# Input norm by token tiles with early first weights, and time steps from 16 stationary columns

## What is computed

```python
h = jnp.concatenate([meta, x], axis=1)            # 16 + 512 tokens
u = rmsnorm(h, norm_mix_w[l])                     # y = x * rsqrt(mean(x*x) + 1e-5) * w
proj = u @ w_in[l]                                # 1024 -> 5136 columns
z, xbc, dt_raw, conf_in = jnp.split(proj, [1024, 3072, 3088], axis=-1)
dt = jax.nn.softplus(dt_raw + dt_bias)            # 16 "time steps" per token, one per head
```

## Time and profile before

| | |
|---|---|
| Median of 3 runs | 3473.9 us (3464.41 to 3475.84) |
| The profiled execution, its own time | 3469.46 us |
| Its span, first to last instruction | 3467.0 us |
| Mean granted TensorE clock | 0.953 |
| Busy: PE, DVE, ACT, POOL | 92%, 77%, 52%, 21% of the span |
| Norm stage ends, projection stage starts | 31.71 us, 32.47 us |
| First matmul of the projection | 44.89 us |

### The profile page before, as it was taken

The page is one execution under the profiler, slowest core; times in us unless marked ns, Lnnn a source line. Parts: engine busy times, 40 slices in busy tenths (PEclk is TensorE's granted clock), DMA queues, the critical chain, the costliest instruction groups (busy, mean ns, idle before and its releaser), DMA issues. The chain is left out here.

```text
span 3467.0 us, 48111 instructions
## 1 busy us (share of the span) xinstructions
PE 3181.1 (92%) x16551; PEld 2746.6 (79%) x16551; DVE 2685.4 (77%) x3820; ACT 1815.5 (52%) x2180; POOL 738.5 (21%) x460
## 2 busy tenths in 40 slices
PE   5999778999897999999999778799999999999996
PEld 5987666899887888888888656688878878888783
DVE  5786554697297778888878455899989999999993
ACT  3343342334486333333333233578777778777772
POOL 0000001345412444454444000011111111111110
PEclk8899788999999999999999889899999999999997
DMA  4221031244455999999897204699989999999993
GB/s 131 62 74 31 1 122 61 95 137 146 170 208 227 342 338 341 346 353 361 330 352 285 101 10 173 251 359 360 357 338 357 364 343 375 360 363 379 355 348 126
DMA packets 195387, 851.96 MB, mean 246 GB/s; under 512 B 21730, under 2 KB 104290, under 8 KB 151572
## 3 DMA queue, kind: packets, MB, share of 16 engines
q1 hardware_dynamic: 167348, 699.56, 55.0%
q0 software_dynamic: 27936, 151.02, 10.7%
HBM read 809.09 MB, written 59.24 MB: 250 GB/s over the span
## 5 line engine op out<-in xcount | busy, mean ns | idle before, releaser
L2889 DVE TENSOR_TENSOR moe_w_lo<-all_raw,moe_w_hi 128x2048 fp32r<-128x2048 f32 x298 | 676.7, 2288 | 60.2 <-ACT moe_w_hi L2830 57.7
L2830 ACT ACTIVATE moe_w_hi<-all_raw 128x2048 fp32r<-128x2048 f32 x298 | 568.4, 1915 | 79.8 <-PE moe_GU L2796 61.7
L2796 PE MATMUL moe_GU<-moe_w_hi,moe_x_lo 128*128 128x512 f32 x1056 | 411.9, 390 | 0.0
L2795 PE MATMUL moe_GU<-moe_w_lo,moe_x_hi 128*128 128x512 f32 x1056 | 411.9, 390 | 0.0
L2794 PE MATMUL moe_GU<-moe_w_hi,moe_x_hi 128*128 128x512 f32 x1056 | 411.5, 390 | 0.0
L1153 POOL TENSOR_TENSOR score_w_lo<-all_hT,score_w_hi 128x1024 fp32r<-128x1024 f32 x68 | 167.4, 2463 | 707.1 <-ACT score_w_hi L1218 707.1
L1781 DVE SCALAR_TENSOR_TENSOR experts_pair<-experts_pair,all_x_first 128x1024 f32<-128x1024 f32 x128 | 156.5, 1223 | 129.7 <-DMA experts_pair<-in_peer_pairs,experts_slot 129.6
L1630 POOL DMA_INDIRECT experts_pair<-in_peer_pairs,experts_slot x128 | 223.0, 1742 | 114.7 <-POOL experts_slot L1627 110.1
L2795 PEld LDWEIGHTS moe_GU<-moe_w_lo,moe_x_hi 128*128 128x128 f32 x1056 | 198.5, 188 | 42.0
L2796 PEld LDWEIGHTS moe_GU<-moe_w_hi,moe_x_lo 128*128 128x128 f32 x1056 | 198.5, 188 | 41.6
L2794 PEld LDWEIGHTS moe_GU<-moe_w_hi,moe_x_hi 128*128 128x128 f32 x1056 | 198.8, 188 | 40.6
(11 more groups left out here) (495 smaller groups left out, 8130.4 us busy)
## 6 DMA issues: line engine op xcount, KB each, us to landing
all_raw<-in_w_moe SPq DMA_DIRECT2D x149, 2048.0 KB, 9.3
all_hT<-in_w_moe SPq DMA_DIRECT2D x49, 2048.0 KB, 9.5
all_hT<-in_peer_wdT SPq DMA_DIRECT2D x128, 512.0 KB, 7.3
all_wu<-in_peer_pairs SPq DMA_DIRECT2D x64, 1024.0 KB, 10.5
peer_gates<-gates_out SPq DMA_DIRECT2D x6, 4096.0 KB, 11.7
experts_gt<-peer_gates SPq DMA_DIRECT2D x32, 768.0 KB, 10.0
all_hT<-in_w_in SPq DMA_DIRECT2D x40, 512.0 KB, 3.8
all_hid<-peer_early SPq DMA_DIRECT2D x60, 192.0 KB, 7.9
```

The costliest lines, as they stand in the source:

```text
L2795: pe.matmul(out, x_hi[:, kx, :], lo[:, k, :], start=False, stop=False)
L2796: mm = pe.matmul(out, x_lo[:, kx, :], hi[:, k, :], start=False, stop=(kx == KD - 1))
L2830: act.activation(w_hi[p % RING][:], piece_of(r, p), ACT.Copy).then_inc(w_high, 1)
L2889: dve.tensor_tensor(w_lo[p % RING][:], piece_of(r, p), w_hi[p % RING][:].bitcast(F32), ALU.subtract).then_inc(w_low, 1)
```

## The change

It has three parts.

1. **Norm tile by tile.** The meta tile is loaded first. For each tile ScalarE squares, VectorE forms the mean, ScalarE the root, VectorE the reciprocal, and ScalarE (not VectorE) scales the tile, before the next tile is squared. A one-element root ahead of everything names the table that ScalarE uses.
2. **First weights beside it.** The first four weight loads of the projection are issued in the norm stage, behind the tokens. They lie in `c.hT`, which the norm stage does not use, under semaphores that live through both stages. VectorE's wait for the small constants moves behind its four first `low_part`s.
3. **Time steps with 16 stationary columns.** 48 matmuls of 264 moving columns stand ahead of job 6; ScalarE copies the result (16 rows by 528 tokens), and ahead of job 10 TensorE turns it by five transposes into the layout of before. `dt_start`, Exp and Ln, and `dt_finish` stand later: behind `low_part(13)`, ahead of job 11's output, and behind part 3 of round 2.

```diff
@@ stage_norm_in @@
+                sp.dma_start(x[0:META, M, :], a["meta_tokens"]).then_inc(loaded[M], 16)
                 for m in range(M):
                     sp.dma_start(x[:, m, :], tokens(a["x"][0])[:, m, :]).then_inc(loaded[m], 16)
-                sp.dma_start(x[0:META, M, :], a["meta_tokens"]).then_inc(loaded[M], 16)
-                sp.dma_start(wn[:], a["norm_mix_w"]).then_inc(wn_in, 16)
+                    if m == 0:
+                        sp.dma_start(wn[:], a["norm_mix_w"]).then_inc(wn_in, 16)
+                for i, at in enumerate(FIRST_COLUMNS):
+                    sp.dma_start(first_weights(c, i), rows(a["w_in"][0])[:, :, at:at + P]).then_inc(c.w_in[i], 16)
...
+                def scale(j, m):
+                    n = P if m < M else META
+                    act.wait_ge(meaned, j + 1)
+                    act.activation(root[0:n, m:m + 1], ss[0:n, m:m + 1], ACT.Sqrt).then_inc(rooted, 1)
+                    act.wait_ge(inverted, j + 1)
+                    act.activation(x[0:n, m, :], x[0:n, m, :], ACT.Copy, scale=root[0:n, m:m + 1]).then_inc(scaled, 1)
...
+                for j, m in enumerate((M, *range(M))):
+                    squares(j, m)
+                    scale(j, m)
+                    if j >= 1:
+                        high_parts(j - 1)
+                high_parts(M)
...
                 for i in range(2 * (M + 1) + 1):
+                    if i % 2 == 0 and 2 <= i < 2 * M:
+                        root_of(i // 2 + 1, i // 2)
@@ stage_project @@
-    DT_JOB = 7
+    DT_JOB, DT_TURN = 6, 10
...
-                for n in range(RING):
-                    load(n)
...
-                    pe.wait_ge(*released(DT_JOB - 4))
-                    for m in range(M + 1):
-                        n, at = (META, 0) if m == 0 else (P, META + (m - 1) * P)
-                        out = ps[0:n, 7, 16 * m:16 * m + 16]
-                        for k in range(KD):
-                            hi, lo = c.u_hi[:, k, at:at + n], c.u_lo[:, k, at:at + n]
-                            pe.matmul(out, hi, wdt_hi[:, k, :], start=(k == 0), stop=False)
-                            pe.matmul(out, hi, wdt_lo[:, k, :], start=False, stop=False)
-                            mm = pe.matmul(out, lo, wdt_hi[:, k, :], start=False, stop=(k == KD - 1))
+                    pe.wait_ge(*released(DT_JOB - 3))
+                    for k in range(KD):
+                        for left, right in ((wdt_hi, c.u_hi), (wdt_hi, c.u_lo), (wdt_lo, c.u_hi)):
+                            for h in range(2):
+                                mm = pe.matmul(ps[0:HEADS, 6 + h, 0:HALF], left[:, k, :], right[:, k, h * HALF:(h + 1) * HALF],
...
+                        t = pe.transpose(ps[0:n, 7, 16 * m:16 * m + 16], flat[:, at:at + n], c.ident[0:HEADS, 0:HEADS])
+                    t.then_inc(dt_turned, 1)
...
                     if n == DT_JOB:
                         project_dt()
+                    if n == DT_JOB + 1:
+                        pe.wait_ge(dt_out, 1)
+                    if n == DT_TURN:
+                        turn_dt()
+                    if n == DT_TURN + 1:
                         pe.wait_ge(dt_raw, 1)
...
-                    if n == DT_JOB + 1:
+                    if n == DT_JOB:
+                        act.wait_ge(dt_done, 1)
+                        act.activation(dtT[:], ps[0:HEADS, 6:8, 0:HALF], ACT.Copy).then_inc(dt_out, 1)
+                    if n == DT_TURN + 1:
...
-                dve.wait_ge(consts_in, 96)
...
                 for n in range(RING):
                     low_part(n)
+                dve.wait_ge(consts_in, 96)
...
+                        if n == DT_TURN + 3:
+                            dt_start()
...
-                        if i == 1 and part == 1:
-                            dt_start()
-                        if i == 2 and part == 1:
+                        if n == DT_TURN + 7:
                             dt_finish()
```

More of the change, by code:

```diff
@@ L123, in stage_norm_in @@
         ut = s.sb("ut", [P, 2, 4, P])
+        warm = s.sb("warm", [P, 1])
         tp = s.ps("tp", [P, 4, 4, P])
@@ L126, in stage_norm_in @@
         wn_in = s.sem("wn_in")
-        cleared, squared, rooted, scaled = (s.sem(n) for n in ("cleared", "squared", "rooted", "scaled"))
-        chain, turned, copied, high, low = (s.sem(n) for n in ("chain", "turned", "copied", "high", "low"))
+        squared, meaned, rooted, inverted, scaled = (s.sem(n) for n in ("squared", "meaned", "rooted", "inverted", "scaled"))
+        turned, copied, high, low = (s.sem(n) for n in ("turned", "copied", "high", "low"))
         def part(i):
@@ new lines, in high_parts @@
+                def high_parts(j):
+                    for i in (2 * j, 2 * j + 1):
+                        n, ks, cols = part(i)
+                        act.wait_ge(copied, i + 1)
+                        act.activation(c.u_hi[:, ks, cols], ut[:, i % 2, :, 0:n], ACT.Copy).then_inc(high, 1)
+                for j, m in enumerate((M, *range(M))):
[4 more added lines that the diff above has]
+                high_parts(M)
@@ L161, in _, with root_of @@
             @block.vector
             def _(dve):
[L163 to L169, removed]
-                    n = P if m < M else META
-                    dve.tensor_scalar(x[0:n, m, :], x[0:n, m, :], ss[0:n, m:m + 1], None,
-                                      ALU.mult).then_inc(scaled, 1)
+                def root_of(j, m):
+                    n = P if m < M else META
+                    v, w = ss[0:n, m:m + 1], root[0:n, m:m + 1]
+                    dve.wait_ge(squared, j + 1)
+                    dve.tensor_scalar(v, v, 1.0 / D, EPS, ALU.mult, ALU.add).then_inc(meaned, 1)
+                    dve.wait_ge(rooted, j + 1)
+                    dve.reciprocal(w, w).then_inc(inverted, 1)
@@ L221, in stage_project @@
     LAST = ROUNDS - 1
-    DT_JOB = 7
+    DT_JOB, DT_TURN = 6, 10
     RING = 4
     with Stage(nc, "proj") as s:
-        w = [c.hT[:].rearrange("p k t -> p (k t)")[:, i * D:i * D + D].rearrange("p (k n) -> p k n", k=KD)
-             for i in range(RING)]
+        w = [first_weights(c, i) for i in range(RING)]
         spare = c.h[:].rearrange("p m d -> p (m d)")
@@ L249, in stage_project @@
         ps = s.ps("ps", [P, 8, 512])
-        w_in_sem = [s.sem(f"w_in{b}") for b in range(RING)]
+        w_in_sem = c.w_in
+        s.sems += c.w_in
         high, low, dt_high, dt_low = (s.sem(n) for n in ("high", "low", "dt_high", "dt_low"))
@@ L281, in load @@
                     sp.dma_start(w[n % RING], w_in[:, :, column(n):column(n) + P]).then_inc(w_in_sem[n % RING], 16)
-                for n in range(RING):
-                    load(n)
+                assert tuple(column(n) for n in range(RING)) == FIRST_COLUMNS
                 sp.dma_start(wdt[:], w_in[:, :, COL_DT:COL_DT + HEADS]).then_inc(consts_in, 16)
@@ L3079, in program @@
                 c.front(front)
+                c.w_in = [nc.alloc_semaphore(f"w_in{i}") for i in range(4)]
                 with ExitStack() as tmp:
```

22 lines of the change are left out of this document (17 added, 5 removed).

## The result

The changed kernel takes 3437.05 us (median of 4 runs, 3430.19 to 3443.89), beside 3469.15 for the kernel before in the same comparison (4 runs, 3464.05 to 3475.84): ratio 0.9902, 95% interval 0.9876 to 0.9928, some 34 us less by the ratio and 32 by the medians. It is faster, as forecast, but by more: the forecast was 3449.0, 24.85 us less, and the median lies only 1 us above the lower end of the stated range, 3436.

What follows compares the result with a forecast made beforehand. VectorE was taken to bound plain projection rounds, with delays in the norm, first weights and time steps. 12.2 + 14.65 - 2.0 = 24.85 us off 3473.9 gave 3449.0, range 3436 to 3460.

Steps and rivals of the forecast that it cites:

- The norm: Norm stage: tiles handled one by one end it at 29.5 instead of 31.71, 2.2 us earlier.
- The upper bound of the working: Norm stage: end at 32.5 if each tile takes 0.7 us more, a loss of 0.8.
- The first weights: Start of the projection: first matmul at about 32.7 instead of 44.89, 12.2 us with the norm's 2.2 in it.
- The large table and the weights behind it: Projection start: convolution table and weights of jobs 4 and 5 come late; counted nothing, up to 2 us in the range.
- The time steps: Projection, round 1: 48 matmuls replace 120 small ones; gate 2 at 124.7 instead of 139.34, 14.65 us won.
- Exp and Ln: Projection, round 2: on ScalarE they now stand ahead of a split VectorE takes; 2.0 us lost.
- The sum: Whole kernel: 12.2 + 14.65 - 2.0 = 24.85 us less.
- A: New time-step block: the clock drops there too, costing 6.2 us, total 3455; chance 0.12.
- B: Norm stage: the tile loop saves nothing, norm ends at 32.5, gain 19.9 us, total 3454; chance 0.08.
- C: Projection start: early weights don't help, tiles or weights come late; with A's clock drop gain 8.6, total 3465; chance 0.08.
- D: TensorE from the time steps on: the low clock stays for the jobs behind, slower, total 3492; chance 0.04.
- VectorE needs 34.23 in a plain round: Projection, plain rounds: VectorE needs 34.23 us gate to gate, TensorE's five jobs 29.35, so VectorE sets the pace.

Runs made afterwards that it cites:

- the repeat: The changed kernel run again without an edit: 3440.55 us (6 runs) beside 3470.49 for the kernel before, ratio 0.992.
- only_dt: The kernel before with part 3, the new time steps, alone: 3450.55 us in one execution.
- narrow_66: The changed kernel with its 48 time-step matmuls of 264 moving columns cut into 192 of 66: 3459.82 us in one execution.
- the five single-part runs: Single executions with only some of the change: only_wait 3471.7 us, only_norm 3455.48, only_weights 3475.46, only_dt 3450.55, no_dt 3450.0.
- late_expln: The changed kernel with Exp and Ln moved from ahead of job 11's output to behind job 14's split: 3431.35 us in one execution.
- narrow_22: The changed kernel with its 48 time-step matmuls of 264 moving columns cut into 576 of 22: 3459.95 us in one execution.
- only_weights: The kernel before with the first weights fetched in the norm stage and the wait for the constants moved, norm as before: 3475.46 us in one execution.
- only_wait: The kernel before with only VectorE's wait for the small constants moved behind its four first remainders: 3471.7 us in one execution.
- only_norm: The kernel before with part 1, the norm tile by tile, alone: 3455.48 us in one execution.
- no_dt: The changed kernel with the time steps of before, including the old places of dt_start, Exp and Ln and dt_finish: 3450.0 us in one execution.

## Why the prediction was right in kind, and the step of it that failed

The mechanism of all three parts was as forecast. The step that failed is a term of the sum, the norm's: 2.2 us, with every high half at its full time on ScalarE between two tiles and 0.5 us more of waits at the end. It measured 4.2 us at the end of the norm stage and 4.4 at the first matmul with the norm alone. With it the forecast gain, 24.85, was too small: 27.3 us were won in the projection stage, and the medians of the totals say 32 and 30. What of these 30 to 32 lies behind the projection stage stays open; it is inside the scatter of the totals.

**The norm, the term that was mis-sized.** Forecast end 29.5, measured 27.52. The last tile was scaled at 22.53 and not 23.8, and what follows took 4.99 us and not 5.7. Of the 1.3 us up to there, half are the start: the meta tile's square started at 5.42 where I took 6.0; I had bounded it by the first token tile of before, which had 128 rows. The chain of a tile was right, 2.97 forecast and 2.94 measured (8.25 to 11.19), though the scaling took 1.15, near the upper of my bounds, and the small steps less. Most of the rest are high halves. I had put 0.4 us for the meta tile's between two tiles; ScalarE's next square started 0.19 after the scaling's end (11.19 to 11.38). I had put 1.26 for a token tile's; it was 0.95 behind tile 1 (14.32 to 15.27). Behind tile 2 it was 1.39, with a wait of 0.33 for VectorE in it, the one such wait ahead of the last scaling. In the tail VectorE took one part every 1.39 us (22.66, 24.05, 25.44), as in the second half before, and lost nothing to high halves: the 0.5 that I had added was not there. The scaling itself: its 1.15 stands 0.09 over the plain copy's 1.06. The Trainium skill ("ScalarE: Activation LUTs", What ACT_TABLE_LOAD costs) puts about 93 ns on each operand of one value per partition; the trace agrees, and a reader could have taken 1.15 from it. The upper bound of the working, 32.5, doesn't follow from 0.7 us more for each of five tiles, which gives 33.0; nothing measured came near it.

**The first weights, right.** From the norm's end to the first matmul I had 3.2 us, and it took 3.23. The large table and the weights behind it cost nothing, as counted; ScalarE's 2.40 us for job 4's weights end at 41.86, and job 1's output, at 44.65, waits for TensorE. One reading was off without a price: ScalarE wants the small constants not at job 0's output but ahead of it, right behind its four splits, and waited 0.57 us for them there. With the true norm the sum for both parts is 14.1, not 12.2. Gate 1 stood at -14.5, 0.4 more, but at -14.1 in the repeat, so the 0.4 is scatter.

**The time steps, right.** Forecast 14.65, measured 14.82 in the changed kernel and 14.78 in *only_dt*. The block took one job's time at full clock, TensorE set the round by 2.6 (3 forecast), and Exp and Ln gave back 2.04 of a forecast 2.0. What I took for a fixed price, 19.8 us with the edges of my stretch, is a block of 17.0 to 19.3 us, by when its clock fell; beside a block of 17.1 the part would be worth 2.2 us less. The drain of about 1.38 us that the Trainium skill ("ScalarE: Activation LUTs", What ACT_TABLE_LOAD costs) adds to a switch of tables isn't there in the changed kernel either. In ScalarE's timeline load, function and load stand back to back:

```profile
114.50 1.28 ACT L411 ACT_TABLE_LOAD   x1
115.80 0.27 ACT L411 ACTIVATE proj_e<-proj_e 128x80 f32<-128x80 f32 x1
116.08 1.28 ACT L413 ACT_TABLE_LOAD   x1
117.38 0.27 ACT L413 ACTIVATE proj_e<-proj_e 128x80 f32<-128x80 f32 x1
117.67 1.28 ACT L432 ACT_TABLE_LOAD   x1
```

**The sum.** At gates 3 to 7 it is 14.1 + 0.4 + 14.8 - 2.0 = 27.3 us against a forecast of 24.85, and 2.0 of the 2.4 between them are the norm. Then 1.2 went again behind gate 7. Ahead of that, TensorE stops for VectorE once more, for 4.6 us in the changed kernel and 3.2 before, and the clock is low at its restart or within a microsecond behind it; in the changed kernel it stayed low longer. Two stretches of four us from about that restart on, first of the changed kernel, then of the kernel before:

```profile
257.00:261.00 4.00, 3.39 (x15) 0.50 0.49 129
261.00:265.00 4.00, 4.00 (x25) 0.67 0.27 73
```

```profile
284.00:288.00 4.00, 3.06 (x16) 0.69 0.46 129
288.00:292.00 4.00, 4.00 (x31) 0.88 0.18 41
```

The clock shares make that some 6.6 us at the low level against some 3.4. From gate 7 to job 39 it took 19.0 us; before, in the repeat, in *narrow_66* and in the five single-part runs it took 17.6 to 17.9. *late_expln* (18.8) and *narrow_22* (19.1) had the long form too, the latter behind a stop of 3.3 us, so the length of the stop doesn't decide it. Since the changed kernel itself shows both, it is scatter between executions; whether the change makes the long form more frequent, three cases don't say. At the program's end the profiled execution stood 25.6 ahead, so that my 24.85 looked exact there: a norm 2 us too dear and a scatter of about that size had cancelled. That is luck, and against the medians it doesn't hold.

**The rivals.** A (the clock drops in the new block) fell: PEclk 1.00. My argument against it, that the moving operand is as long as a job's, is borne out by *narrow_22*, where it is short and the clock fell. The argument for it, that 16 of 128 columns are filled, found no support: the new block and *narrow_66* fill 16 and stayed at 1.00. B fell with a chain of 2.94 us for a tile against 2.97; C fell with ScalarE released by the barrier at 28.30, *only_weights* at -9.6 and an old norm stage that the transfers didn't lengthen; D had no low clock to stay. One reading of the profile ahead of the prediction was too quick, though no term of the sum hangs on it: "VectorE needs 34.23 in a plain round". It gets by with 30.8; the rest was a wait for ScalarE, and some 16 to 17 us lay there over the rounds.

## What to carry to other kernels

- When a stage starts late, undo its waits from the one that ends last. Behind the constant stood the transfer, and behind that the norm: the three pieces gave 5.6, 4.0 and 4.4 us at the first matmul, and moving the first took no more than a line. Then look at the next mark: of the 5.6 alone only 3.9 reached gate 1, where the next transfer was late.
- A loop whose pace "is" one engine may hold a wait on another that comes once a round. Look for it at the idle time ahead of each entry of that engine, and see whether what the other engine does first there can stand later: here it gave 3.4 us in each plain round.
- Put the long operand on the moving side. The same product cost 17.0 to 19.3 us as 120 matmuls with 16 moving columns, 5.9 as 48 with 264 and 6.3 as 192 with 66, and the price of the first form changes from run to run.

## What the runs showed of the hardware that was not expected

- In the old time steps the granted clock fell to 0.50 (1.2 GHz) at a different moment of the same work, with TensorE busy throughout: 2.7 us after its start in two runs, 4.8 to 5.2 in three others. In the new form, over its whole block, it fell after 4.2 us with 22 moving columns (17.1 us), and not at all with 66 (6.3 us) or 264 (5.9 us).
- A matmul of 16 moving columns started 0.03 us behind the one before where 16 stationary columns were loaded for it, and 0.11 where 128 were, both at full clock; at 0.50 the second was 0.21. With 22 on 16 it was 0.026 at full clock and nearly the same at 0.50.
- The issue of the same small load, `proj_wdt`, took SyncE 1.74 us in three runs in which four loads of 0.5 MB had just been issued (before, *only_wait*, *only_norm*) and 0.37 in three in which these had been issued in the norm stage (the changed kernel, *no_dt*, *only_weights*). That the queue's fill is the cause is a guess; no run varied it alone.
- Behind the stop of 3.2 us of TensorE near the stage's end the clock stayed low for some 3.4 us in the kernel before, and behind one of 4.6 us for some 6.6 in the changed kernel, 1.2 us of difference by job 39; in *narrow_22* a stop of 3.3 us was followed by the long form too.
